# A two-layer encoder on one core: the long convolution with folded meta tokens and an even/odd-lag filter transform, and the last expert's work placed ahead of a branch

## The reference

```python
def hyena_mixer(u, ...):
    p = conv_centred(u @ w_in + b_in, conv_w, conv_b)
    x0 = p[..., :D_HYENA]
    x1 = p[..., D_HYENA:2 * D_HYENA]
    v = p[..., 2 * D_HYENA:] * x1
    k = hyena_filters(T, ...)            # 2T lags: hf for i >= 0, hb for i < 0, divided by sum |k|
    fv = jnp.fft.rfft(v.astype(F32), n=2 * T, axis=1)
    fk = jnp.fft.rfft(k, n=2 * T, axis=0)
    y = jnp.fft.irfft(fv * fk[None], n=2 * T, axis=1)[:, :T]
    y = (y + v.astype(F32) * skip.astype(F32)).astype(u.dtype) * x0
    return y @ w_out + b_out

def moe_swiglu(x, router, wg, wu, wd):
    ...
    for e in range(N_EXPERTS):
        ye = swiglu(xt, wg[e], wu[e], wd[e])
        out = out + ye * gates[:, e:e + 1].astype(xt.dtype)
```

## Time and profile before

| | |
|---|---|
| median of 3 runs (lowest, highest) | 1546.01 us (1545.85, 1552.8) |
| the profiled execution, its own time | 1549.65 us |
| its span (first to last instruction) | 1547.8 us |
| mean granted TensorE clock | 0.986 |
| busy: PE, weight load, DVE, ACT, POOL | 98%, 79%, 45%, 20%, 5% |
| chain that ended last: PE, DVE, DMA, ACT | 93%, 4%, 1%, 1% |

### The profile page before, as it was taken

How to read it: one execution, slowest core, us unless ns; L and a number is a source line. 1 busy time by engine, 2 the same in 40 slices (tenths; PEclk the granted TensorE clock), 3 DMA queues, 4 the chain that set the end, 5 groups by cost and what they waited for, 6 DMA issues and landing times.

```text
span 1547.8 us, 45284 instructions
## 1 busy us (share of the span) xinstructions
PE 1517.7 (98%) x20011; PEld 1221.6 (79%) x20012; DVE 698.9 (45%) x1712; ACT 309.8 (20%) x498; POOL 76.3 (5%) x88
## 2 busy tenths in 40 slices
PE   8999999999999999999999999999999999999997
PEld 6776699999879968787787787787787787777775
DVE  5488546664456662423342432533432422523433
ACT  3275344443246501100000000000000000000002
POOL 0071000000020420000000000000000000000000
PEclk9999999999979999999999999999999999999999
DMA  9322045566305507799999999999999999999991
GB/s 288 120 82 83 27 149 179 165 217 216 109 1 163 163 29 297 275 392 393 392 392 392 387 385 394 384 385 393 384 393 386 386 393 384 389 385 390 389 381 58
DMA packets 221395, 432.13 MB, mean 279 GB/s; under 512 B 9530, under 2 KB 76608, under 8 KB 220896
## 3 DMA queue, kind: packets, MB, share of 16 engines
q1 hardware_dynamic: 217960, 425.34, 75.4%
q10 hardware_dynamic: 3256, 4.06, 0.9%
HBM read 428.33 MB, written 1.05 MB: 277 GB/s over the span
## 4 chain that ended last, share of the span: by engine, by line
PE 93%; DVE 4%; DMA 1%; ACT 1%; issue 1%; SPq 0%; ACTq 0%; DVEq 0%
PE ps L1644 91%; PE ps L1661 1%; DMA ring<-in_ffn_w_down_dram 1%; DVE arena L1054 1%; DVE ehT L1526 0%; DVE ring_lo L1262 0%; ACT ring_hi L855 0%; DVE arena L1196 0%; DMA ktab<-in_k_table_dram 0%; DVE arena L1139 0%; DVE arena L1137 0%; ACT arena L668 0%; DVE arena L1164 0%; DVE arena L1170 0%; DVE xtk_lo L1476 0%
## 5 line engine op out<-in xcount | busy, mean ns | idle before, releaser
L1644 PE MATMUL ps<-raw,xg 128*32 128x384 f32 (+2 forms) x9216 | 525.6, 379 | 0.0
L1644 PEld LDWEIGHTS ps<-raw,xg 128*32 128x32 f32 x9216 | 390.6, 110 | 115.0 <-ACT xg L987 0.2
L1644 PE MATMUL ps<-raw,ehT 128*32 128x384 f32 (+2 forms) x4608 | 267.1, 379 | 3.5 <-DVE ehT L1526 3.5
L1526 DVE STREAM_TRANSPOSE ehT<-eh 32x96 f32<-32x96 f32 x896 | 241.6, 270 | 61.9 <-PE ps L1644 32.1
L1514 DVE TENSOR_TENSOR eh<-esg,ps 128x384 f32<-128x384 f32 x56 | 31.0, 554 | 504.0 <-PE ps L1644 485.2
L1644 PEld LDWEIGHTS ps<-raw,ehT 128*32 128x32 f32 x4608 | 203.2, 110 | 53.0 <-issue 4.3
L981 ACT ACTIVATE esg<-ps 128x384 f32<-128x384 f32 x56 | 27.4, 489 | 673.0 <-PE ps L1644 673.0
L1644 PE MATMUL ps<-xn_hi,ring_hi 128*128 128x272 f32 x544 | 159.8, 294 | 0.9 <-DVE crd L1374 0.8
L1644 PE MATMUL ps<-xn_hi,ring_lo 128*128 128x272 f32 x544 | 158.4, 291 | 0.0
L1644 PE MATMUL ps<-xn_lo,ring_hi 128*128 128x272 f32 x544 | 157.7, 290 | 0.0
L1644 PE MATMUL ps<-xn,ring 128*128 128x272 f32 (+1 forms) x640 | 155.7, 403 | 0.9 <-DVE xn L1054 0.8
(11 more groups left out here) (293 smaller groups left out, 1195.9 us busy)
## 6 DMA issues: line engine op xcount, KB each, us to landing
raw<-in_moe_w_gate_dram SPq DMA_DIRECT2D x96, 1024.0 KB, 15.5
raw<-in_moe_w_up_dram SPq DMA_DIRECT2D x96, 1024.0 KB, 14.8
raw<-in_moe_w_down_dram SPq DMA_DIRECT2D x96, 1024.0 KB, 13.9
raw_ring<-in_moe_w_down_dram SPq DMA_DIRECT2D x16, 1024.0 KB, 14.0
raw_ring<-in_moe_w_gate_dram SPq DMA_DIRECT2D x16, 1024.0 KB, 15.2
raw_ring<-in_moe_w_up_dram SPq DMA_DIRECT2D x16, 1024.0 KB, 15.7
ring<-in_w_in_ab_dram SPq DMA_DIRECT2D x12, 1024.0 KB, 6.7
ring<-in_hy_w_in_dram SPq DMA_DIRECT2D x12, 1024.0 KB, 5.0
```

The lines of the kernel that those rows point to most:

```text
L1526: V.transpose(ehT[GROUP * q:GROUP * q + GROUP, s % 2, g, :, :], src).then_inc(sem("ehT_ready"), 1)
L1644: return nc.tensor.matmul(o, l, r, start=start, stop=stop)
```

## The change

It has two halves. In the convolution, the filter's lags are taken as even lags and odd lags (instead of the first and the second 128), and only 128 frequencies are transformed: for each of cosine-even, cosine-odd, sine-even, sine-odd one product, with the other 128 frequencies made on POOL by four sums and differences. The 16 meta tokens are folded into 128 rows (`v_plus` with the sign of the cosine, `v_minus` with that of the sine, made by DVE as two copies and two small operations), so that `vspec` has two products a tile. `vx` moves one block later; the product buffer is doubled; the norm adds the even and odd lags on POOL first and has two products a channel block. DVE's products wait for POOL's eight `filter_sums`; the first product for `kn` waits for four of them.

In the experts, the reading of `more` and the branch go behind the last item's downs (PE) and behind `result` (ACT, DVE); the residual turns go between the last two pairs of downs; SP issues the last four down units and the final weight ahead of its branch; the skipped loop has another body (`later`). At the turn from item 3 to item 4 DVE copies the gathered tiles ahead of the last stage's transposes. The constant table is 1024 columns shorter.

```diff
-        prod = area(12672, 4, 512)
+        prod = [area(12672, 4, 512), area(14864, 4, 512)]
+        spare = area(4608, D)
+        KR_at, KI_at = (KR[:, 0, :], spare), (KI[:, 0, :], KR[:, 1, :])
+        v_plus, v_minus = (ktab[:, K_FIRST + D * i:K_FIRST + D * i + D].rearrange("p (k t) -> p k t", k=KT) for i in range(2))
...
@@ tile order
     add("kn", 0)
-    add("hy", 0, 20)
+    add("hy", 0, 22)
     add("vx", 0, 3)
-    add("hy", 20, 2)
+    add("hy", 22, 2)
     add("vx", 3, 3)
-    add("hy", 22, 2)
     add("vspec", 0, 8)
...
@@ SyncE
+            for s in range(2):
+                for j in range(2):
+                    load_d(NE, 2 * s + j, STAGES - 2 + s, j, NE - 1)
+            sp.dma_start(final_w, A["final_norm"].partition_broadcast(P)).then_inc(sem("final_w_in"), 16)
             sp.wait_ge(sem("later_table"), 1)
             more = sp.value_load(tab[0:1, 0:1], min_val=0, max_val=LATER)
...
@@ GpSimd
-                g(nc.gpsimd.tensor_tensor(kfb[0:n, lt, 0:D], kfb[0:n, lt, 0:D], kfb[0:n, lt, D:2 * D], ALU.add), sem("kabs_sum"))
-
+                g(nc.gpsimd.tensor_tensor(kfb[0:n, lt, 0:D], kfb[0:n, lt, 0:D], kfb[0:n, lt, D:2 * D], ALU.add), sem("filter_sums"))
+            g(nc.gpsimd.tensor_tensor(kfb[:, 0, 0:D], kfb[:, 0, 0:D], kfb[:, 1, 0:D], ALU.add), sem("filter_sums"))
+            pool.wait_ge(used("kspec"), 8)
+            g(nc.gpsimd.tensor_tensor(KR_at[1], KR[:, 0, :], KR[:, 1, :], ALU.subtract), sem("filter_sums"))
+            g(nc.gpsimd.tensor_tensor(KR_at[0], KR[:, 0, :], KR[:, 1, :], ALU.add), sem("filter_sums"))
+            g(nc.gpsimd.tensor_tensor(KI_at[1], KI[:, 1, :], KI[:, 0, :], ALU.subtract), sem("filter_sums"))
+            g(nc.gpsimd.tensor_tensor(KI_at[0], KI[:, 0, :], KI[:, 1, :], ALU.add), sem("filter_sums"))
...
@@ ScalarE
-                if b in (3, 5):
+                if b in (5, 7):
-                    half = b // 2 - 1
-                    for tt, (t0, n) in enumerate(TOKS):
-                        copy("vx", 3 * half + tt, vtok[tt][0:n, 512 * half:512 * half + 512], n, slice(0, 512))
+                    half = b // 2 - 2
+                    for tt in range(3):
+                        copy("vx", 3 * half + tt, vtok[tt][:, 512 * half:512 * half + 512], P, slice(0, 512))
...
             with act.Fori(BATCH, NE) as i:
                 item(i)
+            result(NE, 3)
...
             act.wait_ge(sem("later_table"), 1)
             more = act.value_load(tab[0:1, 0:1], min_val=0, max_val=LATER)
             with act.If(more > 0):
                 with act.Fori(0, more) as j:
-                    gathered(KT * j + 2 * KT, 1)
-                    item(j + NE)
+                    later(j + NE, j)
             sqrt_table()
-            result(more + NE, 3)
...
@@ VectorE
+                if b == 1:
+                    for dst, op in ((v_plus, ALU.add), (v_minus, ALU.subtract)):
+                        v(V.tensor_copy(dst, hyc[:, 8:16, META:META + P]))
+                        v(V.tensor_tensor(dst[:, :, 1:META + 1], hyc[:, 8:16, META + 1:2 * META + 1], hyc[:, 8:16, META - 1::-1], op), sem("v_ready"))
+            dve.wait_ge(sem("filter_sums"), 8)
             for k in range(4):
-                if k >= 1:
-                    dve.wait_ge(sem("spec_ready"), 2 * k)
+                pp = prod[k % 2]
+                if k >= 2:
+                    dve.wait_ge(sem("spec_ready"), 2 * k - 2)
...
@@ VectorE, experts, in item()
+                    if s == STAGES - 1 and between is not None:
+                        between()
                     turn_hidden(i, s, first)
...
-            item(BATCH - 1, then="batch")
-            gathered(KT, BATCH)
+            item(BATCH - 1, then="batch", between=lambda: gathered(KT, BATCH))
...
             item(NE - 1, then="later")
+            result(NE, 3)
...
             more = dve.value_load(tab[0:1, 0:1], min_val=0, max_val=LATER)
...
-            result(more + NE, 3)
             dve.wait_ge(sem("final_w_in"), 16)
...
@@ TensorE, filter
-                close(mm(o[0:n, :], fin[0:64, t0:t0 + n], fw4[0:64, 512 * (k % 4):512 * (k % 4) + 512]))
+                lags = fin[0:64, t0:t0 + n] if k >= 8 else fin[0:64, k // 4:HALF:2]
+                close(mm(o[0:n, :], lags, fw4[0:64, 512 * (k % 4):512 * (k % 4) + 512]))
...
-                for tt in range(2):
-                    last = mm(o[:, :], table[:, tt, f], src[:, tt, 512 * (k % 2):512 * (k % 2) + 512], tt == 0, tt == 1)
-                close(last)
-            pe.wait_ge(sem("kabs_sum"), 3)
+                close(mm(o[:, :], table[:, part % 2, :], src[:, part % 2, 512 * (k % 2):512 * (k % 2) + 512]))
+            pe.wait_ge(sem("filter_sums"), 4)
             o = open_tile("kn", 0)
             for c in range(KT):
-                for tt, (t0, n) in enumerate(TOKS):
+                for tt, n in ((0, P), (2, META)):
...
@@ TensorE, convolution
-                if b in (1, 2):
-                    pe.wait_ge(sem("v_ready"), 1)
-                    for k, (t0, n) in enumerate(TOKS):
+                if b in (2, 3):
+                    pe.wait_ge(sem("v_ready"), 3)
+                    for k, rows in enumerate((v_plus, v_minus, hyc[:, 8:16, META + P:T])):
...
-                for tt, (t0, n) in enumerate(TOKS):
-                    last = mm(o[:, :], (CF, SF)[k % 2][0:n, tt, f], vtok[tt][0:n, 512 * half:512 * half + 512], tt == 0, tt == 2)
+                for tt in range(2):
+                    rows = vtok[2] if tt else vtok[k % 2]
+                    last = mm(o[:, :], (CF, SF)[k % 2][:, tt, f], rows[:, 512 * half:512 * half + 512], tt == 0, tt == 1)
...
@@ TensorE, end
+            down(NE, 0, STAGES * (NE - 1), STAGES - 2)
+            turn_residual(NE)
+            down(NE, 2, STAGES * (NE - 1), STAGES - 1, end=True)
             pe.wait_ge(sem("later_table"), 1)
             more = pe.value_load(tab[0:1, 0:1], min_val=0, max_val=LATER)
             with pe.If(more > 0):
...
                 with pe.Fori(0, more) as j:
-                    item(j + NE)
+                    later(j + NE, j)
+                turn_residual(more + NE)
+
             i = more + NE
-            down(i, 0, STAGES * more + STAGES * (NE - 1), STAGES - 2)
-            down(i, 2, STAGES * more + STAGES * (NE - 1), STAGES - 1, end=True)
-
-            pe.wait_ge(sem("comb_used"), 4 * more + (4 * NE - 4))
...
```

More of the change, by code:

```diff
@@ L593, in _ @@
                 with sp.Fori(0, more) as j:
-                    before = sp.value_load(tab[0:1, bass.ds(j + 1, 1)], min_val=0, max_val=NE - 1)
                     e = sp.value_load(tab[0:1, bass.ds(j + 2, 1)], min_val=0, max_val=NE - 1)
-                    item(j + NE, e, before)
-            last = sp.value_load(tab[0:1, bass.ds(more + 1, 1)], min_val=0, max_val=NE - 1)
-            for s in range(2):
-                for j in range(2):
-                    load_d(more + NE, 2 * s + j, STAGES - 2 + s, j, last)
-            sp.dma_start(final_w, A["final_norm"].partition_broadcast(P)).then_inc(sem("final_w_in"), 16)
+                    later(j + NE, e)
             for tt in range(2):
@@ L922, in _ @@
             for k in range(8):
-                ft, half = k // 4, k % 2
-                dst = KR if k % 4 < 2 else KI
-                copy("kspec", k, dst[:, ft, 512 * half:512 * half + 512], P, slice(0, 512))
+                part, half = k // 2, k % 2
+                dst = KR if part < 2 else KI
+                copy("kspec", k, dst[:, part % 2, 512 * half:512 * half + 512], P, slice(0, 512))
             ring_high(B_HY + 1)
@@ L1021, in _, with later @@
                 item(i)
+            result(NE, 3)
+            def later(i, j):
+                gathered(KT * j + 2 * KT, 1)
+                for s in range(STAGES):
+                    if s == 4:
+                        scatter_table(i)
+                    silu(i, s, later_gate_up_at)
+                result(i + 1, 3)
             act.wait_ge(sem("later_table"), 1)
@@ L1574, in later_table, with item @@
                     v(V.tensor_reduce(gate3[:, tt, NE:ITEMS], prod3, AX.X, ALU.add))
-            def item(i, first=False, then=None):
+            def item(i, first=False, then=None, between=None):
                 for s in range(STAGES):
@@ L1603, in _, with later @@
             item(NE - 1, then="later")
+            result(NE, 3)
+            def later(i, j):
+                for c in range(4):
+                    add_result(i, c)
+                gathered(KT * j + 2 * KT, 1)
+                for s in range(STAGES):
+                    if s == 5:
+                        dve.wait_ge(sem("sel_turned"), i + 1)
+                        select(i + 1)
+                        select_gates(i + 1)
+                    hidden(i, s, later_gate_up_at)
+                    turn_hidden(i, s, last_at=(3, 3), at=later_down_at)
+                result(i + 1, 3)
             more = dve.value_load(tab[0:1, 0:1], min_val=0, max_val=LATER)
@@ L1606, in _ @@
                 with dve.Fori(0, more) as j:
```

(35 more changed lines are left out.)

99 lines of the change are left out of this document (54 added, 45 removed).

## The result

Median 1539.14 us over 6 runs (1538.32 to 1540.77) against 1546.1 over 6 runs of the kernel before; ratio 0.9947, 95% interval 0.9934 to 0.996. Forecast: 1538.4, range 1532 to 1544. The sum of the forecast was -7.65 us, the medians moved by -6.96. The two profiled executions moved by more, 1547.85 to 1537.23 of span, -10.62: the one of before lay 3.6 us above its own median. Where those 3.6 us may lie is what many of the experiments ask.

The account below looks back on a forecast made before the run. PE, busy 98% of the span, was taken as the bound; -9.9 + 0.95 + 1.0 - 2.4 + 2.7 = -7.65 us, from the median 1546.01 to 1538.4 us, range 1532 to 1544.

Parts of the forecast that it names:

- `vspec`: Convolution's vspec: two products instead of three, tiles at 1.72 us instead of 2.95, -9.9 us.
- The `vx` turns: Turns one weight block later in hy: waiting for the low part plus folded rows ahead of the next split, +0.95 us.
- The folded rows' copies: DVE's copies before its taps in hy: 1.1 us each for 1024 columns, 0.6 at twice the rate.
- The gathered copies: Turn from item 3 to 4: DVE copies ahead of 16 transposes remove PE's wait, -2.4 us.
- The filter stage: kspec and kn up to hy's release: PE's saving becomes waiting, POOL's sums hold DVE, +1.0 us.
- Rival 1: Filter stage: POOL's sums do not meet DVE, -3.5 instead of +1.0, total 1533.9 us; chance 0.18.
- rival 4: Filter stage: POOL's four sums pass ahead of DVE's split, +9.5 instead of +1.0, total 1546.9 us; chance 0.06.
- `hy` starts at the lower clock level both times, so nothing is gained or lost: Start of hy: clock at 0.50 before and after the change, no difference on average.
- The end: After the last result: read and branch now delay ACT and DVE ahead of the final norm, +2.7 us.
- DVE's 3.7 us from read to next instruction: Kernel's end: DVE's read and branch put its first final product at 1541.8 instead of 1539.04, +2.75 us.
- rival 3: Kernel's end: branch costs DVE as little as ACT, ACT sets the end, +1.75 instead of 2.7, 1537.4 us; chance 0.10.
- PE at nothing, as well hidden: Kernel's end: PE's 3.84 us branch runs while ACT and DVE make the last result, so PE gains nothing.

Follow-up runs that it names:

- fold_only: The kernel before with the folded meta tokens alone (two vspec products, vx a block later), old filter stage, item turn and end: 1537.58 us, ratio 0.994.
- pool_late: The changed kernel with POOL's four filter sums moved behind coefn, nothing left out: 1539.45 us, ratio 0.994 to the kernel before.
- tail_only: The kernel before with the new order of the end alone (last downs, residual turns, then the branch): 1548.28 us, ratio 1.0004.
- fold_between: The kernel before with folded meta tokens and gathered copies ahead of the transposes, without the filter transform and new end: 1532.88 us, ratio 0.9897.
- before_again: The kernel before, unchanged, run once more for a second trace: 1551.61 us, one run.
- filter_only: The kernel before with the even/odd-lag filter transform alone, three vspec products kept: 1550.71 us, ratio 1.0014.
- pe_busy: The changed kernel with idle products on PE in its two waits, before kn and before hy: 1542.72 us, ratio 0.9955 to the kernel before.
- no_branch: The changed kernel without the loop for later items and its reads and branches on PE, ACT, DVE, SP: 1538.45 us, ratio 0.993 to the kernel before.
- after_again: The changed kernel, unchanged, run again beside kernels of its parts on one chip: 1539.63 us, ratio 0.9943 to the kernel before.

## Why the prediction was right, and where it was not

*`vspec`* (-9.9) came out at -9.88, the pitch of the records being the right price and not the span with its modelled tail. fold_only shows that it is worth this by itself.

*The `vx` turns* (+0.95) cost 0.73: the wait for the low part was 0.52 us for the forecast 0.65 (its own times, 522.29 and 521.70, give 0.59), and the next block did not wait. The folded rows' copies took 0.73 and 0.69 us, not 1.1. The Trainium skill's rate ("VectorE: DVE Perf Modes", "The perf-mode tier table"), about 0.6 us by the forecast's own estimate, is the nearer one, and the trace bears it out for a copy of 1024 float32 columns.

*The gathered copies* (-2.4) brought 2.72. The wait of 2.45 is counted from the modelled end of the product ahead of it; from start to start PE lost 2.6 there, and 0.1 in the first product behind it.

*The filter stage* (+1.0) measured +1.22 against the profiled execution, and each link of the chain was there: PE's wait for the copy, the norm stretched by POOL's fourth sum, the split and `coefn` by its filter sums. Rival 1 fell (the phases did meet), and rival 4 too (POOL held each DVE operation for one sum). pool_late shows the sums' part: moved away, they give 2.6 us back. What is weak is the stage that it was measured against. The forecast took the earlier trace rows as the stage's own time and carried the difference over to a median that lies 3.6 us below that run. Both traces of before have this long stage; with the old stage at 21.0 to 21.2 us, as in three traces of other kernels with the same code there, the step costs 4.0. Which of the two the usual run of before has is not shown.

*"`hy` starts at the lower clock level both times, so nothing is gained or lost"* holds against the first trace of before (6.2 and 6.1 us low) and depends on the same choice. At the start of `hy` the clock is low for 3.0 to 3.5 us in the traces of tail_only, fold_only, fold_between and before_again, and for 5.9 to 6.2 in those of the whole change, filter_only and the first of before. tail_only against the first of before puts that at 1.4 us. pe_busy shows that PE's standing still has a part in it: with PE occupied the clock stays up until `kn`. fold_between, without the transform, has both stretches short.

*The end* (+2.7) was too dear. It is +1.2 against the first trace of before, between +1.6 and -0.4 against all five old ends, and +0.6 by the medians. The step that failed is DVE's 3.7 us from read to next instruction: here it is 1526.48 to 1528.19, at most 1.7, for by then DVE waits for PE. The branch itself takes 56 ns in both traces; in before 2.4 us passed after it, here at most 0.7. That is rival 3, and no_branch shows its mechanism: ACT's table load is last but for 0.45 us. The 2.4 us in before are no fixed price of DVE's branch: with the same code of the end 2.4 to 2.6 us passed in before, before_again and filter_only, and only some 0.5 in fold_only and fold_between. What sets this length was not tried. PE's branch took 3.4 to 3.8 us in all eleven traces that have it. The forecast also put PE at nothing, as well hidden. Its last products came later and ran at the lower clock, which ACT covers by little: PE's product lets DVE start at 1528.25, ACT starts at 1528.51. The Trainium skill's figure of about 0.1 us ("Advanced Engine Details and Errata", "Control Flow Timing") holds for the branch on DVE (0.06), not for PE's (3.8).

So the total came out in part by luck. By the stretches of the table the change is worth -9.4 us against the first trace of before, where the forecast had 1.5 us too much for the end and 0.5 too little gained at the two turns; and it is worth -5.3 against a run with the short filter stage and `hy`, where the forecast had some 4 us too little for these. The medians moved by -6.96 and, beside after_again, by -9.4, as they would if before has both kinds of run in shares that change; that is argued and not shown. The forecast time was right, its -7.65 less well founded than it looks.

What stays open: whether and how often a run of before has the short filter stage (only traces show the stage, and the two of this kernel have the long one), how much of the 3.6 us lies in the start instead, and why the clock falls during `kn`.

## What to carry to other kernels

Halving an engine's work where another chain releases the next stage buys waiting, and on PE the waiting can cost again in the granted clock of what follows; ask first what is last at the stage's end, then test each part of a change alone, for here the kernel without two of its parts was 6.8 us faster by the medians, about 5 of them by the stretches of the trace. Before a trace is used as the baseline of a sum, compare its run with the median, and if they differ, find the stretch that is long before pricing a change in it, and look at the stretches that the change does not touch as well.

## What was not expected of the hardware

A POOL sum of 1024 float32 columns (2.4 us) held a DVE operation with two SBUF inputs for nearly its whole length: `coefn` 2.19 us beside it, 0.29 without. It goes the other way round too: the split of 2048 columns took 2.60 us, 2.29 without, and the sum beside it 4.27. The same code of `kspec` and `kn` took PE from 23.4 us (430.05 to 453.50) to 26.2 (430.57 to 456.76) as the clock was low for 4.1 us of the stage or for 10.3.
